# Half-contraction projections of head 0 placed between the last modulation chunks of a hybrid retention / HGRN2 layer

## The chip, the cores and the metric

The kernel runs on one core of a Trainium2 chip, in one launch. The metric is the device time of that launch in microseconds; the text compares medians of several runs. The engines are named as the profile names them: PE is TensorE's matmul stream and PEld its weight loads, DVE is VectorE, ACT is ScalarE, POOL is GpSimd, SP is the engine whose queue issues all of this kernel's DMAs.

## What is computed

One layer of a bidirectional mixer is applied to 128 context tokens and 512 latent tokens, 640 in all, of width 2048. Everything is float32. The input projection has nine parts of 1024 columns (eight heads of 128 each), and its operand depends on a modulation that has itself to be computed first, from `w_ada`:

```python
shift, scale, gate = jnp.split(mod, 3, axis=-1)      # mod = silu(c) @ w_ada + b_ada, 3 x 2048
h = rms_norm(x, norm_w)
h = h * (1.0 + scale[:, None, :]) + shift[:, None, :]
proj = h @ w_in
rq, rk, rv, rg, hq, hf_f, hf_b, hi, hg = jnp.split(proj, N_IN_PARTS, axis=-1)
...
o_r = merge(rms_norm(o_rf + _flip(o_rb))) * jax.nn.silu(rg)
...
out = jnp.concatenate([o_r, o_h], axis=-1).astype(x.dtype) @ w_out
x = x + (gate[:, None, :] * out).astype(x.dtype)
```

`rq`, `rk`, `rv` and `rg` feed a retention scan, the other five a gated linear recurrence (HGRN2). Context and latent tokens have modulations of their own. The outputs are the two normalised token arrays and the four final states of the context.

## The kernel before

**Stages.** A first stage (0 to about 110 us) loads the tokens, normalises and transposes them, and computes the modulation. A second runs head by head over the input projection, with the scans of the head before woven in, and a last one does the output projection.

**Modulation.** The shift and scale thirds of `w_ada` come in 32 chunks of 1 MB (`load_ada`), in two groups of 16. Group 0 gives shift and scale for the first half of the 2048 contraction rows (tiles k = 0 to 7), group 1 for the second (k = 8 to 15). The chunks rotate through four slots: the load of chunk c waits on `a_used` of chunk c - 4, which PE raises when `ada_chunk` has used it. When a group is complete, DVE copies the row out of PSUM (L892), PE transposes it (`modulation_columns`, L1330), DVE forms the columns (L896, L900) and then `inputs(group)` modulates the eight tiles (L907), ACT rounds each to its high part `hT_hi` (L559), and the low part `hT_lo` comes from DVE for even k (L912) and from POOL for odd k (L1293). Another 16 chunks of 1 MB, the gate third of `w_ada`, are loaded and multiplied (`gate_chunk`, L1367) during head 0.

**Projection.** Each head has nine parts, each of two half contractions of eight tiles: 18 chunks, n = 0 to 17, where part i = n // 2 and half = n % 2. SP loads a chunk of `w_in` (512 KB) into one of three `raw` slots (L390), ACT rounds it to `w_hi` (L573), DVE subtracts to `w_lo` (L932), and PE does 48 matmuls: eight tiles, three products (hi x hi, hi x lo, lo x hi), and each over 640 tokens as two matmuls of 320 columns into two PSUM banks (L1389). `proj(i)` is banks 0 and 1 for even i, 2 and 3 for odd i. Banks 4 to 7 are named A, BB, C, DD.

**Order.** Every engine has its own hand-written loop over n: `chunk`, `gate_chunk`s and `stage` on PE, `split` and then `items(n - 1)` on ACT and DVE, `load` and `items(n)` on SP. Each engine works strictly in that order, and semaphores (`wt_hi`, `wt_lo`, `wt_used`, the `r_...` and `h_...` signals) tie them. ACT and DVE split chunk n only when PE has finished chunk n - 2. When a part is complete, ACT copies it out of PSUM (L637 for part 0 at n = 2, and so on every second n); for part 3, the SiLU gate, ACT takes the exponential and DVE does 1 + e, two reciprocals of half a row each (L937, at n = 8 and n = 9) and the product with the part itself (L1039). The table `freed` says which signal PE waits for before a part overwrites its banks: part 5 waits on the fourth `r_silu`, that last product.

Of the kernel before, what the change touches and what calls it, by code (L numbers as in the profile page):

```python
# [57 lines left out]
ADA_BANKS = (0, 6)  # L58
GATE_SLOTS = 3
GATE_STEPS = 12  # L60
# [31 lines left out]
def layer(nc, x_prompt, x_sample, s_ret_f, s_ret_b, s_hg_f, s_hg_b, c, c_ctx, norm_w, w_ada, b_ada,  # L92
# [3 lines left out]
    with ctx:  # L96
# [209 lines left out]

        def halves(ap):
            return ap.rearrange("p (s n) -> p s n", s=2)
# [26 lines left out]
        def gate_chunks(n):  # L335

            return range(n * KT // GATE_STEPS, (n + 1) * KT // GATE_STEPS) if n < GATE_STEPS else range(0)
# [9 lines left out]
        def _(sp):  # L347
# [26 lines left out]
            for c_ in range(ADA_CHUNKS):  # L374
                load_ada(c_)
# [5 lines left out]
            def load(h, n):  # L381
# [7 lines left out]
                i, half = n // 2, n % 2  # L389
# [9 lines left out]
            def items(n, h, prev):  # L399
# [14 lines left out]
                if n == 6 and h is not None:  # L414
# [6 lines left out]
                if n == 9 and h is not None:  # L421
# [19 lines left out]
            def head(h, prev):  # L441
                for n in range(CHUNKS):
                    load(h, n)
                    items(n, h, prev)

            head(0, None)
# [76 lines left out]
        def _(act):  # L523
# [51 lines left out]
            def projected(h, i):  # L575
                act.wait_ge(wt_used.sem, wt_used.at(h, 2 * i + 2))
# [7 lines left out]
            def items(n, h, prev):  # L584
# [48 lines left out]
                if n == 2:  # L633
# [3 lines left out]
                    act.activation(halves(rq), proj(0), ACT.Copy).then_inc(r_q.sem, 1)  # L637
                if n == 4:
                    projected(h, 1)
                    act.activation(halves(rk), proj(1), ACT.Copy, scale=DK_SCALE).then_inc(r_k.sem, 1)  # L640
                if n == 6:
                    projected(h, 2)
                    act.activation(halves(rvT), proj(2), ACT.Copy).then_inc(r_v.sem, 1)
                if n == 8:
# [3 lines left out]
                    act.activation(halves(rsg), proj(3), ACT.Exp, scale=-1.0).then_inc(r_eg.sem, 1)  # L648
                if n == 10:
# [3 lines left out]
                    act.activation(halves(hq), proj(4), ACT.Copy).then_inc(h_q.sem, 1)  # L653
# [47 lines left out]
            def head(h, prev):  # L701
                for n in range(CHUNKS):
# [3 lines left out]
                    if prev is None and n == 1:  # L706
# [83 lines left out]
        def _(dve):  # L790
# [148 lines left out]
            def items(n, h, prev):  # L939
# [86 lines left out]
                if n == GATE_STEPS and prev is None:  # L1026
# [3 lines left out]
                if n == 8:  # L1030
# [5 lines left out]
                if n == 9:  # L1036
                    reciprocal_half(rsg, 1, r_silu)
                    dve.wait_ge(r_silu.sem, r_silu.at(h, 3))
                    v.tensor_tensor(halves(rsg), halves(rsg), proj(3), ALU.mult).then_inc(r_silu.sem, 1)  # L1039
# [273 lines left out]
        def _(pe):  # L1313
# [60 lines left out]
            def chunk(h, n):  # L1374
# [282 lines left out]
```

## Time and profile before

| | us |
|---|---|
| median of 3 runs | 1628.9 |
| lowest, highest | 1627.71, 1629.46 |
| the profiled execution, device time | 1626.53 |
| its span in the trace | 1624.7 |
| PE busy in the span | 1535.6 (95%) |
| DVE, ACT, POOL busy | 843.5, 483.7, 384.8 |
| mean granted TensorE clock | 0.983 |

The span is what the trace covers; 1.8 us of the profiled execution lie around it. The views used below are: the page (totals of each engine, the share of each line in the chain that ended last), the table of stretches (busy time, clock and DMA share in each), the timeline (instructions in order of time, merged where alike, with the idle time before them and what ended it), the chain in order of time, and the groups by shape. The start of a row is in microseconds from the start of the span.

### The profile page before, as it was taken

What the parts mean: (1) busy time and instruction counts of PE and PEld (TensorE: products, weight loads), DVE (VectorE), ACT (ScalarE), POOL (GpSimd) and SP (SyncE); (2) the same over time, 40 slices, a digit from 0 to 9 for tenths busy, and PEclk for the clock granted to TensorE, in tenths of its full rate; (3) what the DMA queues carried; (4) which work ended last, traced back from release to release, by engine and by line L of the source; (5) the groups of instructions that cost most, each with busy time, mean ns of one, the idle gap of its engine ahead of it and who ended that gap; (6) DMA issues with size and microseconds to landing.
All of it is one profiled execution on the core that took longest, in us unless ns stands there. A gap on an engine that the chain in (4) does not pass through costs nothing.

```text
span 1624.7 us, 24135 instructions
## 1 busy us (share of the span) xinstructions
PE 1535.6 (95%) x9761; PEld 1387.5 (85%) x9761; DVE 843.5 (52%) x1068; ACT 483.7 (30%) x656; POOL 384.8 (24%) x300
## 2 busy tenths in 40 slices
PE   2769999999999999999999999999999996899996
PEld 0238898999999899989998999899999986778884
DVE  2532264556456645645564557355635565752345
ACT  3212123313432332233233323332333224322233
POOL 0110001520251036013501430152025104501220
PEclk9879999999999999999999999999999999999998
DMA  9996821322222222212221222132222114245235
GB/s 359 409 383 211 269 69 56 93 65 77 67 82 65 77 68 82 74 56 83 79 77 56 87 72 77 56 93 66 77 67 82 59 31 163 90 143 194 82 113 207
DMA packets 194803, 187.44 MB, mean 115 GB/s; under 512 B 7344, under 2 KB 163200, under 8 KB 191120
## 3 DMA queue, kind: packets, MB, share of 16 engines
q1 hardware_dynamic: 194704, 185.92, 34.8%
q8 instruction: 86, 1.41, 0.4%
q14 instruction: 13, 0.11, 0.0%
HBM read 169.43 MB, written 12.27 MB: 112 GB/s over the span
## 4 chain that ended last, share of the span: by engine, by line
PE 85%; DMA 5%; issue 4%; DVE 3%; ACT 1%; SPq 1%; POOL 1%; DVEq 0%; POOLq 0%; ACTq 0%
PE ps L1389 60%; DMA area<-in_w_ada 4%; PE ps L1522 4%; PE ps L1524 4%; PE ps L1523 4%; PE ps L1433 3%; PE ps L1488 1%; PE ps L1478 1%; PE ps L1367 1%; PE ps L1437 1%; DVE w_lo L1137 1%; PE ps L1322 1%; PE ps L1490 1%; DMA area<-in_w_in 1%; DMA area<-in_w_out 1%
## 5 line engine op out<-in xcount | busy, mean ns | idle before, releaser
L1389 PE MATMUL ps<-hT_hi,w_hi 128*128 128x320 f32 x2304 | 539.4, 315 | 2.1 <-issue 2.1
L1389 PE MATMUL ps<-hT_hi,w_lo 128*128 128x320 f32 x2304 | 525.2, 309 | 0.0
L1389 PE MATMUL ps<-hT_lo,w_hi 128*128 128x320 f32 x2304 | 524.6, 309 | 0.0
L932 DVE TENSOR_TENSOR w_lo<-area,w_hi 128x1024 fp32r<-128x1024 f32 x144 | 176.5, 1226 | 491.9 <-ACT w_hi L573 491.9
L1389 PEld LDWEIGHTS ps<-hT_hi,w_hi 128*128 128x128 f32 x2304 | 382.0, 188 | 16.8 <-issue 16.8
L1389 PEld LDWEIGHTS ps<-hT_lo,w_hi 128*128 128x128 f32 x2304 | 385.3, 188 | 0.0
L1389 PEld LDWEIGHTS ps<-hT_hi,w_lo 128*128 128x128 f32 x2304 | 385.0, 188 | 0.0
L573 ACT ACTIVATE w_hi<-area 128x1024 fp32r<-128x1024 f32 x144 | 152.2, 1057 | 665.5 <-PE ps L1389 639.6
L937 DVE RECIPROCAL area<-area 128x320 f32<-128x320 f32 x64 | 137.6, 2150 | 1.1
L1522 PE MATMUL ps<-w_hi,hT_hi 128*128 128x512 f32 x320 | 126.8, 396 | 8.2 <-DVE w_lo L1137 8.1
L1262 POOL TENSOR_TENSOR area<-area 128x320 f32<-128x320 f32 x56 | 87.3, 1559 | 192.0 <-ACT area L619 192.0
L1524 PE MATMUL ps<-w_hi,hT_lo 128*128 128x512 f32 x320 | 125.1, 391 | 0.0
L1523 PE MATMUL ps<-w_lo,hT_hi 128*128 128x512 f32 x320 | 125.1, 391 | 0.0
L619 ACT ACTIVATE area<-area 128x1280 f32<-128x1280 f32 x56 | 71.3, 1273 | 153.9 <-DVE area L979 131.2
L1137 DVE TENSOR_TENSOR w_lo<-area,w_hi 128x1024 fp32r<-128x1024 f32 x40 | 54.3, 1357 | 107.8 <-ACT w_hi L739 107.7
L1281 POOL TENSOR_TENSOR area<-area 128x512 f32<-128x512 f32 x16 | 20.3, 1292 | 333.0 <-DVE area L1061 333.0
L1258 POOL TENSOR_TENSOR area<-area 128x320 f32<-128x320 f32 x56 | 70.6, 1261 | 82.5 <-PE ps L1437 82.5
L1322 PE MATMUL ps<-area 128*32 128x512 f32 x256 | 45.8, 800 | 46.0 <-DMA area<-in_w_ada 45.9
L982 DVE TENSOR_TENSOR area<-area 128x640 f32<-128x640 f32 x56 | 46.2, 825 | 80.8 <-ACT area L619 80.8
L1245 POOL TENSOR_TENSOR area<-area 128x1280 f32<-128x1280 f32 x8 | 23.7, 2964 | 271.6 <-ACT area L699 271.6
L739 ACT ACTIVATE w_hi<-area 128x1024 fp32r<-128x1024 f32 x40 | 42.3, 1057 | 134.9 <-PE ps L1524 127.8
L1522 PEld LDWEIGHTS ps<-w_hi,hT_hi 128*128 128x128 f32 x320 | 60.5, 189 | 23.2 <-DVE w_lo L1137 11.0
(210 smaller groups left out, 1571.7 us busy)
## 6 DMA issues: line engine op xcount, KB each, us to landing
area<-in_w_in SPq DMA_DIRECT2D x144, 512.0 KB, 3.7
area<-in_w_ada SPq DMA_DIRECT2D x48, 1024.0 KB, 8.6
area<-in_w_out SPq DMA_DIRECT2D x40, 512.0 KB, 3.6
area<-in_x_sample SPq DMA_DIRECT2D x8, 1024.0 KB, 7.3
out<-area SPq DMA_DIRECT2D x5, 1024.0 KB, 4.7
o_scratch<-area SPq DMA_DIRECT2D x15, 320.0 KB, 4.2
area<-o_scratch SPq DMA_DIRECT2D x15, 320.0 KB, 6.3
area<-area SPq DMA_DIRECT2D x64, 64.0 KB, 2.4
```

The source lines that it names most:

```text
L573: act.activation(w_hi[:, n % 2, :], raw[:, n % 3, :], ACT.Copy).then_inc(wt_hi.sem, 1)
L619: act.activation(x, x, ACT.Exp).then_inc(xe.sem, 1)
L932: v.tensor_tensor(w_lo[:, n % 2, :], raw[:, n % 3, :], w_hi[:, n % 2, :].bitcast(F32), ALU.subtract).then_inc(wt_lo.sem, 1)
L937: v.reciprocal(part, part).then_inc(signal.sem, 1)
L1137: v.tensor_tensor(w_lo[:, m % 2, :], raw[:, m % 2, :], w_hi[:, m % 2, :].bitcast(F32), ALU.subtract).then_inc(d_lo.sem, 1)
L1258: g.tensor_tensor(x[:, :, left], bf[:, :, half - 1:half].broadcast_to([P, nblk, half]), bf[:, :, left], ALU.subtract)
L1262: g.tensor_tensor(x[:, :, left], x[:, :, left], kf[:, :, left], ALU.mult)
L1322: i = mm(ps[g * QUAD:(g + 1) * QUAD, ADA_BANKS[group], :], cs[:, k, :], ada_raw[:, slot, g * WIDE:(g + 1) * WIDE], start=k == 0, stop=k == ...
L1389: ins = mm(out[s], wt[:, n % 2, w], x[:, k, s * HALF:(s + 1) * HALF], start=k == 0 and step == 0, stop=k == KT - 1 and step == 2)
L1522: mm(out, hT_hi[:, k, tile_cols(t)], w_hi[:, m % 2, w], start=k == 0, stop=False)
L1523: mm(out, hT_hi[:, k, tile_cols(t)], w_lo[:, m % 2, w], start=False, stop=False)
L1524: return mm(out, hT_lo[:, k, tile_cols(t)], w_hi[:, m % 2, w], start=False, stop=k == KT - 1)
```

## The change

The second group of modulation chunks (c = 16 to 31) is no longer multiplied in one piece. After three of every four of these chunks PE does a third of a half contraction of head 0: parts 0 to 3, first half (k = 0 to 7, for which group 0 suffices). A fifth half contraction, that of part 4, follows the transposes of group 1. Then come the second halves of parts 0 to 4, and from n = 10 on the order is the old one. The `w_in` chunks that this takes are loaded between the `w_ada` chunks: three before group 1, one each after its eighth and twelfth chunk, one after the last.

Parts 0 to 3 must now all stay open in PSUM at once. Their latent tokens (512 columns) take a bank each (2, 3, A, C), their context tokens (128 columns) a quarter each of bank BB. So for these four parts, in both halves, each pair of matmuls of 320 + 320 columns becomes a pair of 512 + 128 columns. Group 1's row moves from bank 6 to bank 7. The gate chunks stand at n = 5 to 12, two after each chunk, where they stood at n = 0 to 11. ACT and DVE take parts 0 to 3 out together at n = 9, each with a 512-column and a 128-column instruction.

The diff, cut to its core:

```diff
-ADA_BANKS = (0, 6)
+ADA_BANKS = (0, 7)
+AHEAD = 5
-GATE_STEPS = 12
+GATE_STEPS = range(AHEAD, 13)
...
+        def first_head(h):
+            return isinstance(h, int) and h == 0
+        def ahead(h, i):
+            return first_head(h) and i < AHEAD - 1
+        def ahead_parts(i):
+            return ps[:, (2, 3, A, C)[i], :], ps[:, BB, tile_cols(i)]
+        def order(h, n):
+            if first_head(h) and n < 2 * AHEAD:
+                return n % AHEAD, n // AHEAD
+            return n // 2, n % 2
+        def used_by(h, i):
+            return 2 * AHEAD - 1 if ahead(h, i) else 2 * i + 2
+        def moved_at(h, i):
+            return 2 * AHEAD - 1 if ahead(h, i) else 2 * i + 2
...
+            each = KT // len(GATE_STEPS)
+            return range((n - AHEAD) * each, (n - AHEAD + 1) * each) if n in GATE_STEPS else range(0)
...
-            for c_ in range(ADA_CHUNKS):
+            for c_ in range(KT):
                 load_ada(c_)
...
-                if n == 6 and h is not None:
+                if h is not None and n == (8 if first_head(h) else 6):
+                    if first_head(h):
+                        sp.wait_ge(wt_used.sem, wt_used.at(0, AHEAD + 1))
...
-                if n == 9 and h is not None:
+                if h is not None and n == (11 if first_head(h) else 9):
...
+            for n in range(3):
+                load(0, n)
+            for c_ in range(KT, ADA_CHUNKS):
+                load_ada(c_)
+                if c_ == KT + 7:
+                    load(0, 3)
+                if c_ == KT + 11:
+                    load(0, 4)
+            load(0, AHEAD)
             head(0, None)
...
+            def part_out(h, i, dst, func, **how):
+                if ahead(h, i):
+                    lat, context = ahead_parts(i)
+                    act.activation(dst[:, P:T], lat, func, **how)
+                    return act.activation(dst[:, 0:P], context, func, **how)
+                return act.activation(halves(dst), proj(i), func, **how)
...
-                    if prev is None and n == 1:
+                    if prev is None and n == AHEAD:
                         for k in range(ADA_K, KT):
                             high_input(k)
...
-                if n == GATE_STEPS and prev is None:
+                if n == GATE_STEPS[-1] and prev is None:
...
-                if n == 8:
+                if n == moved_at(h, 3):
...
-                if n == 9:
+                if n == moved_at(h, 3) + 1:
...
+                    if prev is None and n == AHEAD:
+                        modulation(1)
                     split(h, n)
-                    if prev is None and n == 1:
-                        modulation(1)
+                    if prev is None and n == AHEAD:
                         inputs(1)
...
-            for c_ in range(KT, 2 * KT):
-                ada_chunk(c_)
-            modulation_columns(1)
...
-            def chunk(h, n):
-                i, half = n // 2, n % 2
+            def chunk(h, n, pieces=1, piece=0):
+                i, half = order(h, n)
...
+                if ahead(h, i):
+                    lat, context = ahead_parts(i)
+                    out = ((lat, slice(P, T)), (context, slice(0, P)))
+                else:
+                    out = [(ps[:, 2 * (i % 2) + s, 0:HALF], slice(s * HALF, (s + 1) * HALF)) for s in range(2)]
+                for kk in range(piece * KC // pieces, (piece + 1) * KC // pieces):
...
+                if piece == pieces - 1:
+                    ins.then_inc(wt_used.sem, 1)
...
                 for n in range(CHUNKS):
-                    chunk(h, n)
+                    if not first_head(h) or n >= AHEAD - 1:
+                        chunk(h, n)
...
+            for c_ in range(KT, ADA_CHUNKS):
+                ada_chunk(c_)
+                at = c_ - KT
+                if at % 4 > 0:
+                    chunk(0, at // 4, 3, at % 4 - 1)
+            modulation_columns(1)
             head(0, None)
```

**PE, after the transposes of group 0** (L1330 before and L1383 now are `modulation_columns`, L1322 and L1375 are `ada_chunk`, of which only the first two chunks and the last are shown of before; L1389 and L1449 are projection matmuls). Before:

```order
L1330 MATMUL ps<-con,area 128x128 [waits row_out]
L1330 MATMUL ps<-con,area 128x128 x3
L1322 MATMUL ps<-area 32x512 [waits a_landed0,x_evac_act]
L1322 MATMUL ps<-area 32x512 x3
L1322 MATMUL ps<-area 32x512 [waits a_landed1]
L1322 MATMUL ps<-area 32x512 x3
L1322 MATMUL ps<-area 32x512 [waits a_landed2]
```

Now:

```order
L1375 MATMUL ps<-area 32x512 [waits a_landed1]
L1375 MATMUL ps<-area 32x512 x3
L1449 MATMUL ps<-hT_hi,w_hi 128x512 [waits h_lo_dve,wt_lo]
L1449 MATMUL ps<-hT_hi,w_hi 128x128
L1449 MATMUL ps<-hT_lo,w_hi 128x512
L1449 MATMUL ps<-hT_lo,w_hi 128x128
L1449 MATMUL ps<-hT_hi,w_lo 128x512
L1449 MATMUL ps<-hT_hi,w_lo 128x128
```

The third modulation chunk of group 1 now stands behind projection matmuls, and these wait for the first `w_lo`.

**DVE, from the splits of head 0 to the end of part 3's gate** (L932 and L979 are the splits, L1033 and L1080 the 1 + e, L937 and L984 the reciprocals, L1039 and L1088 / L1089 the product that raises the fourth `r_silu`). Before:

```order
L932 TENSOR_TENSOR w_lo<-area,w_hi 128x1024 [waits wt_hi] x8
L1033 TENSOR_SCALAR area<-area 128x640 [waits r_eg]
L937 RECIPROCAL area<-area 128x320 [waits r_silu]
L932 TENSOR_TENSOR w_lo<-area,w_hi 128x1024 [waits wt_hi]
L937 RECIPROCAL area<-area 128x320
L1039 TENSOR_TENSOR area<-area,ps 128x640 [waits r_silu]
L932 TENSOR_TENSOR w_lo<-area,w_hi 128x1024 [waits wt_hi] x3
```

Now:

```order
L979 TENSOR_TENSOR w_lo<-area,w_hi 128x1024 [waits wt_hi] x5
L1080 TENSOR_SCALAR area<-area 128x640 [waits r_eg]
L984 RECIPROCAL area<-area 128x320 [waits r_silu]
L979 TENSOR_TENSOR w_lo<-area,w_hi 128x1024 [waits wt_hi]
L984 RECIPROCAL area<-area 128x320
L1088 TENSOR_TENSOR area<-area,ps 128x512 [waits r_silu]
L1089 TENSOR_TENSOR area<-area,ps 128x128
L979 TENSOR_TENSOR w_lo<-area,w_hi 128x1024 [waits wt_hi] x2
```

Before, the product stood behind the split of chunk 10, with three splits (11 to 13) behind it; now it stands behind the split of chunk 11, with two.

**PE, where part 5 begins** (L1367 and L1417 are gate chunks). Now:

```order
L1417 MATMUL ps<-area 32x512 [waits g_landed2]
L1417 MATMUL ps<-area 32x512 x3
L1417 MATMUL ps<-area 32x512 [waits g_landed0]
L1417 MATMUL ps<-area 32x512 x3
L1449 MATMUL ps<-hT_hi,w_hi 128x320 [waits r_silu,r_k,wt_lo]
```

The wait on `r_silu` was there before too, at the same chunk; what has moved is the work on DVE that ends it, by one chunk.

## Rows read from the trace of the kernel before

**Rows 1.** The page: span, and the chain that ended last by engine

```profile
span 1624.7 us, 24135 instructions
PE 85%; DMA 5%; issue 4%; DVE 3%; ACT 1%; SPq 1%; POOL 1%; DVEq 0%; POOLq 0%; ACTq 0%
```

**Rows 2.** Table of stretches: busy us and count by engine, clock, DMA share, GB/s

```profile
60.00:80.00 20.00, 13.16 (x87) 3.73 (x85) 15.28 (x29) 7.33 (x12) 7.09 (x4) 0.83 1.03 409
80.00:100.00 20.00, 12.53 (x64) 1.53 (x64) 0.00 (x0) 0.00 (x0) 0.45 (x1) 0.66 1.03 408
```

**Rows 3.** Timeline of PE, 65 to 110 us: start, length, work, idle before it

```profile
68.92 1.06 PE L1322 MATMUL ps<-area 128*32 128x512 f32 x8 [1.28 <-DMA area<-in_w_ada]
...
102.23 1.93 PE L1322 MATMUL ps<-area 128*32 128x512 f32 x8 [1.55 <-DMA area<-in_w_ada]
108.75 1.12 PE L1330 MATMUL ps<-con,area 128*128 128x128 f32 x4 [4.58 <-DVE area L892]
```

**Rows 4.** Timeline of ACT, then of DVE, between the two groups

```profile
78.09 0.74 ACT L559 ACTIVATE hT_hi<-area 128x640 fp32r<-128x640 f32 x1 [1.94 <-DVE area L907]
104.02 1.06 ACT L573 ACTIVATE w_hi<-area 128x1024 fp32r<-128x1024 f32 x1 [25.19 <-DMA area<-in_w_in]
105.78 1.06 ACT L573 ACTIVATE w_hi<-area 128x1024 fp32r<-128x1024 f32 x1 [0.70 <-DMA area<-in_w_in]
...
105.11 1.23 DVE L932 TENSOR_TENSOR w_lo<-area,w_hi 128x1024 fp32r<-128x1024 f32 x1 [26.32 <-ACT w_hi L573]
```

**Rows 5.** The chain in order of time: start, length, work

```profile
109.87 7.96 PE ps L1389 x48
117.83 1.00 PE ps L1367 x8
118.82 7.23 PE ps L1389 x48
...
134.28 1.85 PE ps L1367 x16
...
212.75 14.27 PE ps L1389 x96
...
281.91 7.03 PE ps L1389 x48
...
323.66 0.89 PE ps L1433 x8
```

**Rows 6.** Timeline of PE in the output projection, twelve matmuls apart

```profile
1499.71 0.39 PE L1522 MATMUL ps<-w_hi,hT_hi 128*128 128x512 f32 x1
...
1502.43 0.39 PE L1522 MATMUL ps<-w_hi,hT_hi 128*128 128x512 f32 x1
```

**Rows 7.** Weight loads by shape, 117 to 212 us: busy us, mean ns

```profile
L1389 PEld LDWEIGHTS ps<-hT_hi,w_hi 128*128 128x128 f32 x176 | 29.0, 188 | 9.2 <-issue 9.2
L1367 PEld LDWEIGHTS ps<-area 128*32 128x32 f32 x128 | 2.9, 108 | 4.7 <-issue 4.7
```

**Rows 8.** Timeline of DVE and of POOL: first and last step of `inputs(1)`

```profile
110.47 2.23 DVE L907 TENSOR_SCALAR area<-area,small 128x128 f32<-128x128 f32 x6
...
123.10 1.58 POOL L1293 TENSOR_TENSOR hT_lo<-area,hT_hi 128x640 fp32r<-128x640 f32 x1 [1.39 <-ACT hT_hi L559]
```

**Rows 9.** Timeline of ACT and of DVE around chunk 10's split

```profile
185.46 1.06 ACT L573 ACTIVATE w_hi<-area 128x1024 fp32r<-128x1024 f32 x1 [6.58 <-PE ps L1389]
...
186.55 1.23 DVE L932 TENSOR_TENSOR w_lo<-area,w_hi 128x1024 fp32r<-128x1024 f32 x1 [3.31 <-ACT w_hi L573]
187.69 2.14 DVE L937 RECIPROCAL area<-area 128x320 f32<-128x320 f32 x1
189.87 0.82 DVE L1039 TENSOR_TENSOR area<-area,ps 128x640 f32<-128x640 f32 x1
```

**Rows 10.** Timeline of DVE at the gate row; SP's gate loads, issue to landing

```profile
213.23 0.68 DVE L1029 TENSOR_TENSOR area<-ps,area 128x512 f32<-128x512 f32 x1
...
DMA to landing us min/median/max: 4.6/5.1/14.3
```

More of the change, by code:

```diff
@@ L442, in head @@
                 for n in range(CHUNKS):
-                    load(h, n)
+                    if not first_head(h) or n > AHEAD:
+                        load(h, n)
                     items(n, h, prev)
+            for n in range(3):
[7 more added lines that the diff above has]
+            load(0, AHEAD)
             head(0, None)
@@ L647, in items @@
                         act.wait_ge(r_out.sem, r_out.at(h - 1))
-                    act.activation(halves(rsg), proj(3), ACT.Exp, scale=-1.0).then_inc(r_eg.sem, 1)
-                if n == 10:
+                    part_out(h, 3, rsg, ACT.Exp, scale=-1.0).then_inc(r_eg.sem, 1)
+                if n == moved_at(h, 4):
                     projected(h, 4)
@@ L652, in items @@
                         act.wait_ge(pe_level.sem, pe_level.at(h - 1))
-                    act.activation(halves(hq), proj(4), ACT.Copy).then_inc(h_q.sem, 1)
+                    part_out(h, 4, hq, ACT.Copy).then_inc(h_q.sem, 1)
                 if n == 12 or n == 14:
@@ L1372, in _ @@
                      5: (r_silu, 0, 4), 6: (h_q, 0, None), 7: (h_ez, 0, 1), 8: (h_ez, 0, 2)}
-            def chunk(h, n):
-                i, half = n // 2, n % 2
-                pe.wait_ge(wt_lo.sem, wt_lo.at(h, n + 1))
-                if half == 0:
-                    signal, back, k = freed[i]
-                    if due(signal, h - back, k):
-                        pe.wait_ge(signal.sem, signal.at(h - back, k))
-                out = [ps[:, 2 * (i % 2) + s, 0:HALF] for s in range(2)]
-                for kk in range(KC):
+            def chunk(h, n, pieces=1, piece=0):
+                i, half = order(h, n)
+                if piece == 0:
+                    pe.wait_ge(wt_lo.sem, wt_lo.at(h, n + 1))
+                    if half == 0 and not (first_head(h) and i < AHEAD):
+                        if first_head(h) and i == 5:
+                            pe.wait_ge(r_k.sem, r_k.at(0))
+                        signal, back, k = freed[i]
+                        if due(signal, h - back, k):
+                            pe.wait_ge(signal.sem, signal.at(h - back, k))
+                if ahead(h, i):
+                    lat, context = ahead_parts(i)
+                    out = ((lat, slice(P, T)), (context, slice(0, P)))
+                else:
+                    out = [(ps[:, 2 * (i % 2) + s, 0:HALF], slice(s * HALF, (s + 1) * HALF)) for s in range(2)]
+                for kk in range(piece * KC // pieces, (piece + 1) * KC // pieces):
@@ L1383, in chunk @@
                     k = half * KC + kk
                     w = slice(kk * P, (kk + 1) * P)
-                    if isinstance(h, int) and h == 0 and n < 2:
+                    if first_head(h) and n in (0, AHEAD):
                         pe.wait_ge(h_lo[low_by(k)].sem, h_lo[low_by(k)].at(k // 2))
                     for step, (wt, x) in enumerate(((w_hi, hT_hi), (w_hi, hT_lo), (w_lo, hT_hi))):
-                        for s in range(2):
-                            ins = mm(out[s], wt[:, n % 2, w], x[:, k, s * HALF:(s + 1) * HALF],
-                                     start=k == 0 and step == 0, stop=k == KT - 1 and step == 2)
@@ L1391, in chunk @@
-                ins.then_inc(wt_used.sem, 1)
+                        for bank, cols_of in out:
+                            first = k == 0 and step == 0 and not (ahead(h, i) and i > 0 and cols_of.start == 0)
+                            ins = mm(bank, wt[:, n % 2, w], x[:, k, cols_of],
+                                     start=first, stop=k == KT - 1 and step == 2,
+                                     skip_group_check=ahead(h, i) and cols_of.start == 0)
+                if piece == pieces - 1:
+                    ins.then_inc(wt_used.sem, 1)
@@ L1462, in stage @@
                         pe.wait_ge(gate_ready.sem, gate_ready.at(0))
+                        pe.wait_ge(r_silu.sem, r_silu.at(0))
                     if due(h_out, h - 1, 1):
```

23 lines of the change are left out of this document (13 added, 10 removed).

## The prediction

> **What bounds the kernel now.** I read the page first: the chain that ended last is 85% PE, DMA is 5% [rows 1]. From 110 us on PE hardly ever stops, so a change can gain only before that, or by taking PE work away; this one takes none away. The table of stretches shows the place: from 60 to 100 us the 16 DMA engines are full (share 1.03, 409 GB/s), PE is busy 13 of 20 us, and at a granted clock of 0.83 and 0.66 [rows 2]. The timeline says why: the modulation chunks of group 1 come one every 2.56 us (the 14 from 68.92 to 102.23), PE uses each in 1 us at the 2.4 GHz level, or 1.9 at the 1.2 GHz level, and waits for the next. The first projection matmul follows the transposes at 109.87 [rows 3, 5]. Between 80 and 103 us ACT and DVE are idle (25.19 and 26.32 us before their first splits) [rows 4].
>
> **What the edit does to the start.** PE uses chunks 16 and 17 and then stands at the first projection piece, which waits on `w_lo`. That wait is new, and the 14 remaining modulation chunks are queued behind it, with the loads that need their slots. `w_hi` can't start before ACT has rounded group 0, 78.09 + 0.74 = 78.8 us; then 1.06 (ACT) and 1.2 to 1.4 (DVE): **PE starts at 81.3** [rows 4]. Of group 1, 14 chunks are then still to be used; before it was nine.
>
> Is it DMA or PE that sets the pace from there? A `w_in` chunk costs the queues 1.76 us (104.02 to 105.78) [rows 4], so five of them put the last landing at 102.23 + 5 x 1.76 = 111.0. PE's own work is longer, as the sum below shows (129 us), and each chunk's slot is refilled early enough: gate chunks of the same size land 4.6 to 5.1 us after issue [rows 10], and a slot is wanted again 11 us after it was freed. So PE sets it.
>
> **A 128-column matmul.** The sum hangs on the one shape that the trace doesn't have: a matmul of these operands over 128 columns. At 512 columns the spacing is 2.72 / 12 = 227 ns [rows 6], at 320 it is 7.03 / 48 = 146.5 ns [rows 5]. The line through both (0.417 ns a column and 13 ns fixed) gives **67 ns** at 128; then 227 + 67 = 293 ns, just what 2 x 146.5 costs now. That is the low end. But every matmul loads its weights, and the load has to fit beside the matmul ahead of it. A load of 32 columns lasts 108 ns, one of 128 columns 188 ns [rows 7]: 80 ns for 96 columns, so 128 columns stream in 107 ns. Beside 146 or 227 ns that is hidden, beside 53 ns of a 128-column matmul it isn't. The nearest row is full float32 over 128 columns: 0.89 / 8 = 111 ns an instruction [rows 5]. If the 13 ns come on top of the 107, it is 120. I take **115 ns**, between the two. The high end is that these operands at 128 columns cost what full float32 does, two such instructions, **222 ns** [rows 5].
>
> The Trainium skill (TensorE: Matmul & The Clock Gate, "LDWEIGHTS") puts a weight load at its columns over 1.2 GHz, which is 107 ns for 128 and is the slope of the loads in the trace. The same page ("Back-to-back issue gap") has a sustained stream of loads and matmuls at 81 ns for 128 columns, which no row here shows; what it would make is among the rivals.
>
> At 115 ns a pair is 342 ns and a half contraction 24 x 0.342 = 8.20 us, 1.17 more than 7.03. Eight half contractions have this shape.
>
> **The sum to the end of group 1**, from 81.3. A gate chunk between two projection chunks adds 8.23 - 7.03 = 1.20 us, two together 1.85 + 7.23 - 7.03 = 2.05 [rows 5]; a modulation chunk is the same four matmuls. In the new order 8 stand singly and 3 times two together: 9.6 + 6.15 = 15.75. Four half contractions: 32.8. PE has idled 8 us, and I take it to start at the 1.2 GHz level again, as at 108.75: there the four transposes took 1.12 us where four such instructions take 0.45, and the first chunk 7.96 instead of 7.23 [rows 3, 5], so 1.4. Copy hidden under the last piece, transposes 0.5. 81.3 + 15.75 + 32.8 + 1.4 + 0.5 = **131.8**, against 109.9 now: 21.9 us later.
>
> **The sum from there to the start of chunk 13**, where both orders have done the same work. Now: 212.75 + 14.27 / 2 = 219.9, so 110.0 us after the transposes [rows 5]. After the change:
> - part 4's first half, 7.1, covers the modulation of group 1, but not all. DVE needs 0.6 from the transposes to `inputs`, and the split of chunk 5 (1.3) now stands ahead of it. From its start to POOL's last low part it takes 123.10 + 1.58 - 110.47 = 14.2 [rows 8]. The last tile, 1.0, follows: 17.2 instead of 7.1 + 8.2 = 15.3, **1.9 us of waiting**. In the kernel before, the same steps end before PE wants them.
> - second halves of parts 1 to 3, each with two gate chunks ahead: 3 x (8.20 + 2.05) = 30.8, which makes 47.9.
> - chunk 9: 2.05 + 7.03, 57.0.
> - chunk 10 waits for the fourth `r_silu`. Before, the product came 0.07 + 1.06 + 0.1 + 1.2 + 2.15 + 0.85 = 5.3 us after the end of chunk 8 (185.36 to 190.7) [rows 9], and PE had chunk 9 to do. Now these steps stand behind the end of chunk 9, with no chunk between, only 1.85 us of gate chunks: **3.6 us of waiting**. With the product in two instructions chunk 10 starts 5.45 after chunk 9 and ends at 57.0 + 5.45 + 7.1 = 69.6.
> - chunks 11 and 12: 2 x 9.08, and chunk 12's gate chunks 1.9: 89.7.
>
> 131.8 + 89.7 = 221.5 against 219.9: **+1.6**. Put as a ledger: four half contractions moved forward save 28.1 (4 x 7.03), gate chunks in pairs 17.8 - 16.4 = 1.4, the slow first chunk 0.9; the later end of group 1 takes 21.9, the wider shape after it 4 x 1.17 = 4.7, the two waits 5.5: 32.1 against 30.4.
>
> **Further on.** DVE adds the gate row after the last gate chunk (L1029). That was at 213.23, right when DVE came to it; now the last two gate chunks follow chunk 12, and DVE stands there 8 us with the work of its next items behind it (5.5 us to the end of the split of chunk 14, 6 more to that of 15). By my count these splits come 0.7 and 0.8 us before PE wants them. I put 0.5 us for it, 0 to 2. SP's loads of `w_in` are each behind a gate load's wait, and land 1 to 3 us before ACT wants them; DVE's wanting is some 6 us behind that, except at chunk 11, where lateness would go straight into the 3.6 us wait. The `r_S0` loads and the eight rotary swaps on SP (moved from n = 9 to n = 11) are wanted only 20 us later. ACT's four parts at n = 9 (some 3 us) end before chunk 9 does. Its four extra instructions lie there too.
>
> Sum: +1.6 + 0.5 = +2.1 on the profiled execution's 1626.5 us, that is 1628.6; the median of before is 1628.9, so I forecast **1631**. Heads 1 to 7 and the output projection are untouched.
>
> **The rivals.**
> - *The load hides (under 100 ns).* Each ns of the 128-column matmul costs 24 x 7.1 half contractions = 0.17 us (the one that waits for group 1 hardly counts). At 67 ns that is -8.2: 1622.7. For it: 320 and 512 columns lie on a line without any weight load in it. Against: the loads' own slope, and the 111 ns row. By the skill's 81 ns, 34 less than mine, it would be 5.8 us less, 1625: a gain just above what can be told. The trace has no row for it, and the load time of the same page speaks against it here. I give 12% to a load that hides in full and 8% to one that hides in part.
> - *Slower by much (222 ns).* The short shape falls back to the cost of full float32. The place is every second matmul of the eight half contractions; PE bounds in both stretches, so all is paid: 107 ns x 0.17 = +18, and 0.7 more because group 1 then is no longer what chunk 5 waits for: 1650. It decides as soon as the shape costs 122 ns or more (7 above mine, +1.2 us). For it only that no row of these operands is shorter than 320 columns. 12%.
> - *The waits cascade.* The 3.6 us wait sends the clock to 1.2 GHz (as the 4.58 us of idling ahead of the transposes at 108.75 did, 1.12 us against 0.45) and costs 1.4 more, and late `w_in` loads or DVE's gate row add 2 to 4: 1634 to 1637. Against: PE is dense ahead of that wait, which it wasn't there. 8%.
> - *The change does not do what it says*: the order of instructions shows that it does. Nothing.
>
> **The numbers.** 60% for the forecast, whose own range is 1628 to 1635 (111 to 120 ns, 0 to 2 us further on, the clock's 1.4). A measurement of this kernel tells about 0.2%, 3.3 us, from no change. Faster by more: 17% from the first rival and 3% from mine. Within: 38% from mine, 3% from the first, 1% from the third. The rest slower, 38%. The range of 8 in 10 goes from the first rival's end to the third's, 1621 to 1638; it leaves out the 222 ns case.
>
> **What the profile will show.** The spacing of a 512 + 128 pair, 342 ns, against 293 or 449; first projection matmul at 81.3 us; transposes of group 1 at 131; DMA share under 1 from 85 to 125 us, since PE holds it up; PE idle 3.6 us ahead of the first matmul of part 5, released by DVE's product, and some 2 us within the second half of part 0, released by POOL or ACT; chunk 13 at 221. The forecast is wrong if the pair costs something else, if the first piece starts much after 81, or if a wait stands in head 0 that I haven't named.

## The result, and the profile after

| | before | after |
|---|---|---|
| median, us (9 runs each) | 1628.91 | 1633.34 |
| lowest, highest | 1626.59, 1631.02 | 1630.35, 1634.86 |
| the profiled execution, device time | 1626.53 | 1633.58 |
| its span in the trace | 1624.7 | 1631.8 |
| mean granted TensorE clock | 0.983 | 0.98 |

The ratio after / before is 1.0023, with a 95% interval of 1.0012 to 1.0033: by the ratio the change makes the kernel 3.7 us slower, by the two medians 4.4. The forecast was 1631, that is 2.1 over before.

The page of after: the shares of the chain that ended last. Against [rows 1] the DMA share of the chain fell from 5% to 3%, and behind the first projection piece PE no longer waits for a chunk in head 0; PE's share rose by one.

```profile
PE 86%; DVE 4%; issue 4%; DMA 3%; ACT 1%; POOL 1%; SPq 0%; DVEq 0%; ACTq 0%; POOLq 0%
```

The table of stretches of after (busy us and count of PE, PEld, DVE, ACT, POOL, then granted clock, DMA share, GB/s). It is to be read against [rows 2]. Up to 80 us DMA still sets the pace; then PE stands and takes DMA down with it (a share of 0.18); from 90 on PE is full, with the clock at 1.00. In the last row PE is waiting for group 1's operands and DMA is almost idle.

```profile
80.00:90.00 10.00, 8.06 (x31) 5.32 (x32) 2.85 (x2) 1.08 (x2) 0.80 (x1) 0.58 0.18 55
90.00:100.00 10.00, 10.00 (x67) 6.25 (x70) 1.23 (x1) 1.06 (x1) 0.00 (x0) 1.00 0.84 296
...
140.00:150.00 10.00, 8.64 (x47) 6.88 (x47) 8.98 (x13) 4.59 (x6) 5.58 (x3) 1.00 0.03 11
```

The two long waits that the new order gives PE in after, 60 to 400 us (who waited, for whom: us in total, times, longest). The first is the one for `w_lo` ahead of the first projection piece, the second the one for the fourth `r_silu` ahead of chunk 10.

```profile
PE ps L1449 <- DVE w_lo L979: 7.7, 1, 7.7
PE ps L1449 <- DVE area L1089: 3.7, 1, 3.7
```

The chain of after in order of time (start, length, work). L1375 are modulation chunks, L1449 projection matmuls. The pieces of part 0 come at 81.94, 87.90 and 92.40, the first piece of part 1 at 97.47; the last tile of part 0's second half (n = 5, behind part 4's first half) at 149.70; chunk 13 at 223.43.

```profile
81.94 4.10 PE ps L1449 x12
86.04 1.87 PE ps L1375 x8
87.90 3.50 PE ps L1449 x18
...
92.40 3.22 PE ps L1449 x18
95.62 1.85 PE ps L1375 x16
97.47 2.21 PE ps L1449 x12
...
148.10 1.56 POOL hT_lo L1346
...
149.70 1.24 PE ps L1449 x6
...
196.13 7.27 PE ps L1449 x48
...
223.43 7.23 PE ps L1449 x48
```

The timeline of PE in after (start, length, work, and in brackets the idle time before it and what ended it). The rows at 93.42 and 94.44 are three pairs of 512 + 128 columns apart.

```profile
93.42 0.50 PE L1449 MATMUL ps<-hT_hi,w_hi 128*128 128x512 f32 x2
...
94.44 0.50 PE L1449 MATMUL ps<-hT_hi,w_hi 128*128 128x512 f32 x2
...
132.94 0.60 PE L1383 MATMUL ps<-con,area 128*128 128x128 f32 x4
...
196.13 0.53 PE L1449 MATMUL ps<-hT_hi,w_hi 128*128 128x320 f32 x2 [3.69 <-DVE area L1089]
```

**Where the time went.** Chunk 13 of head 0 starts at 223.43; before it was 212.75 + 14.27 / 2 = 219.9 [rows 5]. That is +3.5, and it is the part that belongs to the edit, give or take half a microsecond: the transposes of group 1 started at 108.75 in before and at 108.91 and 109.31 in two kernels that differ from it only behind them. The two spans differ by 7.1, so 3.6 come later. I followed ACT's splits, which from n = 12 of head 0 on are the same 132 instructions in both: the distance is 3.6 at 266 us and stays 3.6 up to 574; then it grows in five steps, at the starts of heads 3 to 7, to 5.2 at the last split (1326.88 before, 1332.07 after); the last 1.9 come behind it. The steps are PE's idle time between two heads that nothing in the profile releases. There are five of them in every kernel here, and they stand where PE's loop over heads 2 to 7 jumps back; the starts of heads 1 and 2, in front of the first jump, have none. First before, then after, 400 to 1330 us, the same columns as the waits above:

```profile
PE ps L1389 <- issue: 2.1, 5, 0.4
```

```profile
PE ps L1449 <- issue: 3.6, 5, 0.9
```

The last 1.9 come with a lower clock. Two rows of the table of stretches, 1340 to 1400 us, where PE is thinly used between the last head and the output projection: first before, then after. The same place was granted 0.94 in the one and 0.83 in the other.

```profile
1340.00:1400.00 60.00, 43.83 (x233) 37.21 (x232) 38.95 (x53) 27.18 (x37) 32.19 (x26) 0.94 0.42 144
```

```profile
1340.00:1400.00 60.00, 46.04 (x212) 37.83 (x212) 33.82 (x47) 23.61 (x33) 27.29 (x23) 0.83 0.40 136
```

Is either of the two later parts the edit's? After was run again, beside the variants below. In that execution the distance was 3.6 at 266 us, 4.8 at the last split and 4.7 at the end, with the clock at 0.91 from 1340 to 1400. So the 1.9 is a matter of the execution, which one profile can't tell from an effect of the edit. The idle time between heads was 3.3 there, in the kernels derived from after 2.7 to 3.4, in two derived from before 2.4 and 3.1. The groups overlap; what sets its length stays open.

### The profile page after: what moved, and what is told of

It is laid out like the page before. It is cut to its first block, busy times and chain, and to the rows that moved or that the text cites. A ratio compares the mean times of both kernels' runs of the same rounds, so it can differ in the third digit from the quotient of the medians.

```text
span 1631.8 us, 24137 instructions
## 1 busy us (share of the span) xinstructions
PE 1546.8 (95%) x9761; PEld 1394.5 (85%) x9761; DVE 842.5 (52%) x1069; ACT 484.7 (30%) x660; POOL 382.9 (23%) x300
## 4 chain that ended last, share of the span: by engine, by line
PE 86%; DVE 4%; issue 4%; DMA 3%; ACT 1%; POOL 1%; SPq 0%; DVEq 0%; ACTq 0%; POOLq 0%
PE ps L1449 60%; PE ps L1592 4%; PE ps L1593 4%; PE ps L1594 4%; PE ps L1495 4%; DMA area<-in_w_ada 2%; PE ps L1375 1%; PE ps L1551 1%; PE ps L1541 1%; DVE area L954 1%; PE ps L1499 1%; DVE w_lo L1190 1%; PE ps L1417 1%; PE ps L1553 1%; DMA area<-in_w_out 1%
## 5 line engine op out<-in xcount | busy, mean ns | idle before, releaser
L1449 PE MATMUL ps<-hT_hi,w_hi 128*128 128x320 f32 (+2 forms) x2304 | 543.2, 317 | 16.3 <-DVE w_lo L979 7.7
L1449 PE MATMUL ps<-hT_hi,w_lo 128*128 128x320 f32 (+2 forms) x2304 | 528.6, 311 | 0.0
L1449 PE MATMUL ps<-hT_lo,w_hi 128*128 128x320 f32 (+2 forms) x2304 | 528.2, 310 | 0.0
L979 DVE TENSOR_TENSOR w_lo<-area,w_hi 128x1024 fp32r<-128x1024 f32 x144 | 176.8, 1228 | 478.6 <-ACT w_hi L612 478.6
L1449 PEld LDWEIGHTS ps<-hT_hi,w_hi 128*128 128x128 f32 x2304 | 380.2, 188 | 42.3 <-issue 28.7
L1449 PEld LDWEIGHTS ps<-hT_lo,w_hi 128*128 128x128 f32 x2304 | 383.3, 188 | 2.9
L1449 PEld LDWEIGHTS ps<-hT_hi,w_lo 128*128 128x128 f32 x2304 | 383.1, 188 | 2.8
L984 DVE RECIPROCAL area<-area 128x320 f32<-128x320 f32 x64 | 137.6, 2150 | 1.1
L1375 PE MATMUL ps<-area 128*32 128x512 f32 x256 | 41.8, 740 | 34.5 <-DMA area<-in_w_ada 34.4
```

What stands on the lines that cost most here:

```text
L979: v.tensor_tensor(w_lo[:, n % 2, :], raw[:, n % 3, :], w_hi[:, n % 2, :].bitcast(F32), ALU.subtract).then_inc(wt_lo.sem, 1)
L984: v.reciprocal(part, part).then_inc(signal.sem, 1)
L1449: ins = mm(bank, wt[:, n % 2, w], x[:, k, cols_of], start=first, stop=k == KT - 1 and step == 2, skip_group_check=ahead(h, i) and cols_of. ...
```

## Experiments

They ran in two groups, each on one chip beside the kernel before: the wide shape, the widths, the early split and the early product on one (before took 1627.68 to 1631.31), after once more and the three combined versions on the other (1626.77 to 1632.69). The median of before was 1630.42 us in both, so that times of the two groups can be set side by side. Ratios are with 95% intervals; "after" is taken at its 1633.73 of the second group.

### The wide shape alone

This run prices what eight half contractions cost in the shape 512 + 128, with nothing moved. It is the kernel before, with this for head 0, parts 0 to 3:

```diff
-out = [ps[:, 2 * (i % 2) + s, 0:HALF] for s in range(2)]     # 320 + 320 tokens
+out = [(ps[:, 2 * (i % 2), :], slice(P, T)), (ps[:, 2 * (i % 2) + 1, 0:P], slice(0, P))]   # 512 + 128
```

and the evacuations in the same two pieces.

> The kernel before with its old order and banks 0 to 3, but parts 0 to 3 of head 0 computed as 512 + 128 columns, not 320 + 320, and taken out of PSUM in the same two pieces. Nothing else moves. Theory (the 128-column matmul costs 114 ns because its neighbour's weight load does not fit beside it): each of the 8 half contractions takes 24 x 0.341 = 8.19 us for 7.03, all of it on PE's path: 8 x 1.16 = +9.3 us, 1638.2 by the median of before, and 341 ns for a pair in the trace. Rival (most of what the change loses is in its new waits, and the 128-column shape is only dear beside the modulation chunks): under +3 us, 1629 to 1632.

Measured: **1638.82 us** (1637.72 to 1639.97), ratio 1.0056 [1.0043, 1.0070], 8.4 over the median of before against 9.3 expected. The chain of this kernel, in order of time, has the reason. A half contraction of the new shape takes 8.32 where one of 320 + 320 takes 7.24; 48 matmuls each. Chunk 13 starts at 223.05 + 7.14 = 230.2, 10.3 later than before: 8.7 for the shape, 0.6 because the transposes started that much later in this execution, and 1.0 because the first half contraction, at the lower clock, took 10.07 (1.75 over its usual time, where before it was 0.73).

```profile
121.48 8.32 PE ps L1401 x48
...
188.42 7.24 PE ps L1401 x48
...
223.05 14.27 PE ps L1401 x96
```

So the shape costs 1.1 us in each half contraction (8.7 in eight), and it is paid in full: PE bounds here. The rival that the short matmul hides its load is out, for this pair.

### A matmul by width and by weight columns

This run asks why 128 columns cost what they do. It is the kernel before, with the matmuls of head 0's chunks n = 2 to 13 cut to other shapes behind their first k-tile (parts 1 to 6 of head 0 are thus not the reference's):

```diff
+width = {2: (64, P), 3: (96, P), 4: (128, P), 5: (160, P), 6: (192, P), 7: (224, P), 8: (256, P), 9: (288, P),
+         10: (128, 64), 11: (128, 32), 12: (64, 32), 13: (512, P)}.get(n)      # columns, weight columns
```

> The kernel before, where in chunks 2 to 13 of head 0 seven of the eight contraction tiles use other shapes; what these chunks compute is changed by that, so parts 1 to 6 of head 0 are not the reference's. In order: 64, 96, 128, 160, 192, 224, 256, 288 columns with 128 weight columns (chunks 2 to 9), 128 columns with 64 weight columns (10), 128 with 32 (11), 64 with 32 (12), 512 with 128 (13). Only the spacing of the matmuls in the trace is read. Theory (the weight load of the next matmul must fit beside this one: 107 ns for 128 weight columns, and some ns to change over): 64 to 224 columns all cost the same 107 to 118 ns, 256 costs 120, 288 costs 133; with 64 weight columns 128 columns cost about 67, with 32 the same, and 64 columns with 32 weight columns about 40. Rival (a matmul of these operands under 256 columns pays more for each column): time grows with width, 57 ns at 64 columns, 114 at 128, 171 at 192, and falls back at 256; fewer weight columns change nothing.

Measured, from the chain of this kernel, 42 matmuls in a row of each shape: 64, 128, 224, 256 and 288 columns with 128 weight columns; then 128 columns with 64 and with 32 weight columns, 64 with 32, and 512 with 128.

```profile
128.67 4.61 PE ps L1394 x42
...
144.60 4.64 PE ps L1394 x42
...
165.63 4.68 PE ps L1394 x42
172.38 5.03 PE ps L1394 x42
180.34 5.53 PE ps L1394 x42
187.94 2.52 PE ps L1394 x42
192.53 2.52 PE ps L1394 x42
197.97 1.36 PE ps L1394 x42
200.30 9.55 PE ps L1394 x42
```

By 42 that is 109.8, 110.5, 111.4, 119.8 and 131.7 ns, then 60, 60, 32.4 and 227.4 ns. From 64 to 224 columns a matmul costs the same 110 ns; above that it follows the line of 320 and 512 columns. With at most 64 weight columns the 128-column matmul falls to 60 ns. (The run took 1610.43 us in all, which says nothing here.) So the floor belongs to the load of 128 weight columns, and not to the columns that stream: it is neither a fall-back to full float32 (222 ns) nor a fixed cost of a matmul. The Trainium skill (TensorE: Matmul & The Clock Gate, "LDWEIGHTS") puts such a load at its columns over 1.2 GHz, an estimate of 107 ns for 128; the 110 ns measured here agree with it to 3 ns. The 81 ns of its section "Back-to-back issue gap" for 128 columns were reached by no row with 128 weight columns.

### After, once more

After ran again beside the variants, on the same chip, with a second trace.

> The changed kernel itself, again, beside the others on one chip. Theory (the change costs 3.5 us up to the start of chunk 13 of head 0; the rest of the 7.1 us between the two profiled spans is the granted clock in the transition after head 7, 0.83 against 0.94 from 1340 to 1400 us, which differs from execution to execution): 3 to 5 us over the kernel before, and chunk 13 starts at 222 to 224 us in the trace. Rival (the change also slows something later): 6 us or more over it.

Measured: **1633.73 us** (1631.24 to 1635.26), ratio 1.0020 [1.0011, 1.0029], 3.3 over before, inside the 3 to 5 expected; chunk 13 started at 223.34, inside too. The trace differs from the first in two places. The slow stretch at the first piece is shorter: the piece takes 4.10 again, but the modulation chunk behind it 1.12 (1.87 in the first trace) and the second piece 3.21 (3.50). And chunk 10, right behind the 3.7 us wait, is slower. In order: the start, chunk 10 and chunk 13 in the chain, and a row of the table of stretches just behind the wait, in which the granted clock is 0.57.

```profile
81.36 4.10 PE ps L1449 x12
85.46 1.12 PE ps L1375 x8
...
194.50 8.81 PE ps L1449 x48
...
223.34 7.23 PE ps L1449 x48
```

```profile
194.40:198.40 4.00, 3.90 (x16) 0.57 0.82 223
```

In the first trace of after the same stretch, 196 to 200 us, has a clock of 1.00, and chunk 10 takes 7.27. Before the wait PE was dense in both. So a wait of 3.7 us sends the clock to 1.2 GHz in some executions and not in others; where it does, the chunk takes 8.81, 1.5 us more. (It started 1.6 us earlier in this execution, 0.6 of it from the first piece's start and 1.0 from the shorter slow stretch, which is why chunk 13 comes out alike.)

### The first split ahead of group 0's operands

This run tests the price of the wait at 81.94. From after, the first split goes ahead of the work that it waited behind:

```diff
 # ACT
+            split(0, 0)
             for k in range(ADA_K):
                 high_input(k)
 # DVE
+            split(0, 0)
             inputs(0)
 # both, in head 0's loop
-                    split(h, n)
+                    if not (first_head(h) and n == 0):
+                        split(h, n)
```

> The changed kernel with one edit: ACT and DVE split the first w_in chunk ahead of modulating group 0, not behind it. Theory (from 81.9 us on PE sets the pace, and the 7.7 us of idling ahead of it are lost for good): the first projection piece can start at about 73.6, gated tile by tile by the low parts, the first half contraction ends 7 us earlier (88.3 for 95.6) and the whole kernel with it: -7, 1626.3. Rival (DMA sets the pace of group 1 after all, since the last chunk can't land before 111): the head start is eaten by waits for modulation chunks, and under 2 us is gained.

Measured: **1624.90 us** (1622.93 to 1626.06), ratio 0.9968 [0.9956, 0.9980]: 8.8 under after, more than the 7 expected. The chain:

```profile
74.16 3.54 PE ps L1454 x12
77.70 1.00 PE ps L1380 x8
...
86.13 1.85 PE ps L1380 x16
...
186.64 8.64 PE ps L1454 x48
...
215.30 7.23 PE ps L1454 x48
```

The two modulation chunks behind part 0's first half start at 86.13; in after it was 95.62. The pieces begin 7.8 us earlier (74.16 against 81.94), and the rest is the clock: in this kernel the first piece took 3.54 instead of 4.10, and the next modulation chunk 1.00 instead of 1.87. Of 9.5 us won there, 8.1 are left at chunk 13 (215.30 against 223.43): chunk 10 ran at the lower clock again (8.64), as in the second trace of after. The rival, that less than 2 us would come of it because DMA is full up to 80 us, is out.

### The product a chunk earlier

This run tests the price of the 3.7 us wait. From after, part 3's product is made at n = 9, ahead of the split of chunk 11:

```diff
-                if n == moved_at(h, 3) + 1:
+                if n == moved_at(h, 3) + (0 if first_head(h) else 1):
```

> The changed kernel with one edit: for head 0 DVE does both halves of the reciprocal and the product of part 3 in one go at n = 9, ahead of the split of chunk 11, not the second half behind it. Theory (PE's wait of 3.7 us ahead of part 5 is a price of its own): DVE has the product ready at 191.1 us, before PE has finished chunk 9 and two gate chunks (192.5), so the wait goes and the kernel gains 3.6 us: 1629.7. Rival (something else is late right behind it, the split of chunk 11 or the gate row): the wait moves on, and less than 1.5 us is gained, 1632 to 1633.3.

Measured: **1627.39 us** (1625.78 to 1629.41), ratio 0.9984 [0.9975, 0.9993]: 6.3 under after where 4 were expected, and 3.0 under before. The timeline of DVE: both reciprocals stand together, and the split comes behind them.

```profile
185.06 4.17 DVE L984 RECIPROCAL area<-area 128x320 f32<-128x320 f32 x2
...
190.99 1.23 DVE L979 TENSOR_TENSOR w_lo<-area,w_hi 128x1024 fp32r<-128x1024 f32 x1 [0.85 <-ACT w_hi L612]
```

The chain: chunk 9, gate chunks, chunk 10 with no wait between; chunk 13 at 218.92, 4.5 before that of after.

```profile
182.57 7.23 PE ps L1449 x48
189.81 1.85 PE ps L1417 x16
191.66 7.23 PE ps L1449 x48
...
218.92 7.23 PE ps L1449 x48
```

The trace accounts for 4.5 of the 6.3: 3.7 of waiting, and 0.8 from differences ahead of it (the slow stretch at the start took 2.3 here and 3.0 in after). The other 1.8 I can't place; a drop of the clock behind the wait, 1.5 us in those executions of after that have it, would be the right size, but a timed run without a trace doesn't show it.

### Both

The two edits above together, on after:

> The changed kernel with both edits: first split ahead of modulating group 0, and the whole reciprocal and product of part 3 at n = 9. Theory (the two waits of PE, 7.7 and 3.7 us, are separate prices, and the second also made the clock drop in the run with the early split, 1.4 us): chunk 13 starts at 210.5 (215.3 less 3.6 and 1.4), so 9 us under the kernel before, 1620. Rival (they overlap): no better than the early split alone, -5, 1624.

Measured: **1619.67 us** (1618.49 to 1621.23), ratio 0.9935 [0.9921, 0.9948]; chunk 13 at 209.35, 14.1 before that of after, and 14.1 is also the distance of the medians. The gains add: 8.1 + 4.5 = 12.6 from the traces, and the 1.4 that split_early's slow chunk 10 lost (8.64 against 7.23). The chain, at chunk 13:

```profile
209.35 7.23 PE ps L1454 x48
```

No run has the two reorderings without the move. In the trace of before they would have had nothing to win: from 109.87 to 227.03 the chain is PE's work alone, with no wait in it.

### Two parts ahead, in the old shape

Are four open parts needed? With two, PSUM has room for 320 + 320 columns, and no shape changes. From both of the edits above: only parts 0 and 1 between the chunks, in sixths, from the fifth chunk of group 1 on.

```diff
-AHEAD = 5
+AHEAD = 3
-            return ps[:, (2, 3, A, C)[i], :], ps[:, BB, tile_cols(i)]
+            return ps[:, 2 + 2 * i:4 + 2 * i, 0:HALF]
...
-                at = c_ - KT
-                if at % 4 > 0:
-                    chunk(0, at // 4, 3, at % 4 - 1)
+                at = c_ - KT - 4
+                if at >= 0:
+                    chunk(0, at // 6, 6, at % 6)
```

In this version the gate chunks stand at n = 4 to 11, and PE's wait on `r_k` ahead of part 5 is dropped; the product doesn't hold up chunk 10, since part 3 has its old place in the order.

> Another way to do the same: only parts 0 and 1 are computed half ahead, as 320 + 320 columns in banks 2 to 5, in twelve pieces after modulation chunks 20 to 31; part 2's first half covers the modulation of group 1; first split early; the gate chunks at n = 4 to 11. Theory (what the change loses is PE time: the 128-column shape, and more work between the modulation chunks than DMA leaves room for): with 14 us of projection and no dear shape DMA sets the pace again, the transposes of group 1 end at 111.0 (102.2 + 3 x 1.76 for the loads, 3.5 for what follows the last chunk), two half contractions are saved and 2.9 us is waited for the low parts; chunk 13 starts at 208: -12, 1617. Rival (fewer parts ahead save less, 14 us for 28): chunk 13 no earlier than 212, -8 or less, 1621 or more.

Measured: **1618.46 us** (1616.92 to 1620.14), ratio 0.9926 [0.9912, 0.9939]. The chain: DMA again has the last word up to 108.7, the last piece runs behind the last chunk, and chunk 13 starts at 202.25 + 14.27 / 2 = 209.4.

```profile
99.07 9.65 DMA area<-in_w_ada
108.77 1.06 PE ps L1374 x8
109.84 1.97 PE ps L1445 x12
...
202.25 14.27 PE ps L1445 x96
```

It was expected at 208, and 1617 us. Of the 1.4 missing at chunk 13, 1.2 are there at the transposes of group 1: they ended at 112.2 and not at 111.0, since the last modulation chunk landed at 108.7 only. Behind them PE waits for group 1's operands, piece by piece, as in after. That takes 1.8 us in all.

Chunk 13 stands where it stood with four parts ahead (209.35), and the medians are 1.2 apart. So the third and fourth part moved ahead bring nothing: they cover chunks that DMA delivers by 109 anyway, and cost a shape that takes 1.1 us more in each of eight half contractions. One run changes number and shape together, so it doesn't say which of the two weighs more.

### Gate chunks as cover

The same, with two gate chunks at each n from 2 to 9, so that the first ones stand where PE waits for group 1's operands, and the first pair behind a wait for the first low part that DVE makes of group 1. The large constants are loaded two steps later:

```diff
-GATE_STEPS = range(4, 12)
+GATE_STEPS = range(2, 10)
```

> The same with the gate chunks at n = 2 to 9, so that the first two stand in the wait for group 1's low parts, and the large constants loaded two steps later. Theory: 2 us of the 2.9 us wait are filled with work that is to be done anyway: chunk 13 at 206, -14, 1615. Rival (the first gate chunks, loaded behind the last modulation chunk, are not there in time): the wait only changes its releaser, 1617 as without.

Measured: **1617.19 us** (1614.49 to 1617.95), ratio 0.9914 [0.9897, 0.9930], the fastest here: 13.2 us under before, 16.5 under after. One wait of PE is left between 112 and 224 us, 0.5 us long. Chunk 13 starts at 214.02 - 7.1 = 206.9 (four chunks in one, 185.67 to 214.02), against 206 expected. First that wait, then the chain:

```profile
PE ps L1445 <- POOL hT_lo L1345: 0.5, 1, 0.5
```

```profile
185.67 28.35 PE ps L1445 x192
```

Against two_early the median moved by 1.3, and the intervals of the two ratios overlap; chunk 13 moved by 2.5.

## Why the prediction was right, and where its sum was not

**The 128-column matmul** was the term that everything hung on, and it held: a pair took (94.44 - 93.42) / 3 = 341 ns against 342. The argument was right too, not only the number. I had taken 107 ns from the slope of the loads and 111 and 120 as bounds; the floor is 110. My 115 was 5 ns too high, and was made good by the 512-column matmul beside it: 341 less 110 leaves 231 ns for it, where it takes 227 in a row of its own. That the two errors cancel is luck. The low bound, 67 ns, was for a load that hides: 128 columns do run at 60 ns, but only with half the weight columns. The 222 ns rival fell with the same rows.

**The start.** 81.94 instead of 81.3, and 81.36 in the second trace. ACT and DVE took the steps in the forecast order. In the first trace ACT was through with group 0 at 79.19, 0.4 later than in before (78.83), which is as much as executions of one kernel differ there. The first `w_lo` took 1.72, its first 0.6 us beside POOL's last low part, where I had 1.2 to 1.4; `w_hi` took 0.96 where I had 1.06.

**The cold start** is the term that was mis-sized: 1.4 forecast, 3.0 measured. I had read the slow period from the place before the first projection matmul, where the transposes and a part of one chunk were slow [rows 3, 5]. Here the idle time was 7.7 us, and the clock came back later: the first piece took 4.10 (2.21 at 2.4 GHz), the modulation chunk behind it 1.87 (1.00), and the second piece 3.50 (3.22): 1.9 + 0.9 + 0.3, in all 3.0. The granted clock from 80 to 90 us was 0.58. The same sum is 2.0 in the second trace of after and 2.3 in that of the run with the product a chunk earlier, with the same wait ahead. Nor was the 1.4 a fixed price of the place from which I took it: transposes and first chunk together lost 2.4 in the run of the wide shape alone and 1.8 in the run by width. What failed is that one execution's figure was taken for a constant; the traces show a range from 1.4 to 3.0.

**To the end of group 1.** Forecast 131.8; the transposes ended at 132.94 + 0.60 = 133.5. The start gives 0.6 of the 1.7 and the cold start 1.6; 0.5 came back, since the modulation chunks cost less than forecast (12.50 from 97.47 to 109.97, with 12.65 in the sum).

**From there to chunk 13** the steps held almost to the tenth. 89.7 us were forecast and 223.43 - 133.54 = 89.9 measured. Part 4's first half and part 0's second half together ended 17.4 after the transposes (17.2), the last tile behind POOL's last low part, as said; DVE's and POOL's low parts were both among the releasers on the way. The three second halves that follow took 30.5 (30.8). Ahead of chunk 10 PE stood 3.69 (3.6), released by DVE's product, as said. (The terms that led to the 3.6 add up to 5.4 and not 5.3, which changes nothing.)

**Further on.** I had put 0.5 for the gate row and late loads. The distance to before is 3.5 at chunk 13 and 3.6 at 266 us: 0.1. The timeline of DVE in after shows it waiting for the gate row, with the splits behind it early enough:

```profile
223.50 0.69 DVE L1076 TENSOR_TENSOR area<-ps,area 128x512 f32<-128x512 f32 x1 [8.59 <-PE ps L1417]
```

**DMA** was to be under a share of 1 from 85 to 125 us, since PE would hold it up. It was 0.18 from 80 to 90 us, 0.84 up to 100 and then 1.00 to 1.07; from 85 to 125 the mean was 0.88. The sum doesn't use it, but the picture was wrong for the second half of that stretch: from 100 us on the loads of `w_in` and `w_ada` together fill the queues just as fast as PE frees slots.

**The sum** was +1.6 up to chunk 13 and the trace has +3.5. The 1.9 are 0.6 of the start and 1.6 of the cold start, less the 0.5 that came back, and 0.2 in the steps behind. In the second trace of after the same 1.9 are made up otherwise: 0.1 of the start and 0.6 of the cold start, less 0.5, so that group 1 ended at 131.9, as forecast; then the 0.2, and 1.5 for chunk 10 at the lower clock, for which the sum had nothing. The two traces agree on chunk 13 within 0.1 us by different ways. With the 0.5 for further on, of which 0.4 wasn't needed, the forecast was +2.1, and by 266 us it is +3.6. The medians have +4.4 and +3.3 in the two comparisons. The steps at the heads and the clock at the end add 3.5 to the profiled execution, and they aren't in the forecast; of them the medians show little. The range was met: 1633.3 and 1633.7 lie in 1628 to 1635, in its upper half.

**The rivals.** "The waits cascade" was right as a mechanism and misplaced as a rival: the clock does drop behind the 3.7 us wait, in one of two traces of after and in split_early, and costs 1.4 to 1.5 there. It belonged in the forecast as a term with a chance, not beside it. Its other half, late loads, did not happen.

**What the forecast didn't see** is the size of what was left on the table. I took both waits as given, priced them right (the 7.7 us in the late start, the 3.6 us as such), and both come from the place of two instructions in an engine's order. Without them the same change is a gain of 0.65%.

## What to carry to other kernels

A matmul of this kernel's operands with 128 weight columns costs 110 ns however narrow its moving operand is, up to 224 columns, so a split of 640 columns into 512 + 128 cost 341 ns here where 320 + 320 cost 293: keep the halves equal, or shrink the number of parts that have to be open at once. When PE's work is moved under a transfer, ask first whether the engines that prepare its operands get to it in time; here the order on ACT and DVE was worth four times what the move itself cost. Move only as much as the transfer really covers: two half contractions fill the time until DMA is through, and four merely put chunks behind PE. A cost that depends on the clock needs more than one trace: the slow stretch ahead of the first projection work cost anything from 1.4 to 3.0 us.

## What the hardware showed that I had not expected

- With 128 weight columns the time of a matmul hardly depends on its width up to 224 columns (109.8 ns at 64 columns, 111.4 at 224), and halving the weight columns to 64 nearly halves it (60 ns), after which 32 gives nothing more at 128 columns.
- The same wait of 3.7 us, behind equally dense work, is followed by a granted clock of 0.57 in one execution and of 1.00 in another.
- In the thin stretch from 1340 to 1400 us the clock was 0.94, 0.91, 0.89, 0.86 or 0.83, with the span behind the last split 1.0 to 2.4 us longer at 0.89 and below than at 0.91 and 0.94 (with two parts ahead it was 1.0 at 0.83, so the clock is not all of it). A profile of before that lies at the good end makes any other kernel look slower by that.
- Each time PE's loop over the heads jumps back it idles with nothing that releases it: up to 0.4 us in the trace of before and up to 0.9 in after, 2.1 against 3.6 in five. It isn't settled what sets the length.
